# Whole products in layer 0's first projection half, seven half-size products for layer 1's last pair

## What is computed

```python
z = h @ w_in_l                       # h: 264 x 1024, w_in_l: 1024 x 4096
q, k, v, u, g = jnp.split(z, [QK_W, 2 * QK_W, 2 * QK_W + ATTN_W, 2 * QK_W + ATTN_W + POOL_W], axis=-1)
q = rms_norm(q.reshape(B, T, N_HEADS, 2, HEAD_DIM), q_gain)
k = rms_norm(k.reshape(B, T, N_HEADS, 2, HEAD_DIM), k_gain)
g = jax.nn.sigmoid(g.astype(F32)).astype(h.dtype).reshape(B, T, N_BRANCH, D_MODEL)
```

## Time and profile before

| | |
|---|---|
| median of 3 runs | 1595.51 us (1592.43 to 1597.35) |
| the profiled execution's own time | 1594.39 us |
| its span, first to last instruction | 1592.7 us |
| PE busy | 1556.1 us, 98% |
| DVE, ACT, POOL busy | 33%, 12%, 4% |
| first projection half, layer 0 | 34.42 to 102.37 us |
| first projection half, layer 1 | 481.57 to 539.03 us |
| experts of layer 1 | 697.6 to 1575 us |

### The profile page before, as it was taken

How to read it: one execution, slowest core, us unless ns; L and a number is a source line. 1 busy time by engine, 2 the same in 40 slices (tenths; PEclk the granted TensorE clock), 3 DMA queues, 4 the chain that set the end, 5 groups by cost and what they waited for, 6 DMA issues and landing times.

```text
span 1592.7 us, 38054 instructions
## 1 busy us (share of the span) xinstructions
PE 1556.1 (98%) x17094; PEld 975.9 (61%) x17094; DVE 529.0 (33%) x1244; ACT 190.8 (12%) x524; POOL 69.8 (4%) x118
## 2 busy tenths in 40 slices
PE   7999999999999999999999999999999999999997
PEld 3887798999998877944444444444444444445554
DVE  4568267656556672741101101110111011101133
ACT  3123213111112232131000000000000000000000
POOL 1115000000000110010000000000000000000010
PEclk9999999999999999999999999999999999999999
DMA  9998979786359754579999999999999999999995
GB/s 361 358 368 262 302 265 333 262 273 213 128 173 332 243 176 153 174 300 373 413 409 394 417 418 402 418 415 405 418 404 414 417 404 418 416 403 418 409 390 194
DMA packets 174360, 535.43 MB, mean 336 GB/s; under 512 B 12535, under 2 KB 101413, under 8 KB 161394
## 3 DMA queue, kind: packets, MB, share of 16 engines
q1 hardware_dynamic: 158274, 494.58, 81.2%
q0 software_dynamic: 8784, 29.03, 5.5%
q10 hardware_dynamic: 7136, 9.34, 1.8%
HBM read 517.53 MB, written 15.82 MB: 335 GB/s over the span
## 4 chain that ended last, share of the span: by engine, by line
PE 92%; DMA 4%; DVE 3%; ACT 1%; issue 1%; SPq 0%; ACTq 0%; DVEq 0%
PE banks L2107 35%; PE banks L1294 19%; PE banks L2128 17%; PE banks L1651 7%; DMA ring<-in_w_exp_up 3%; PE banks L1570 2%; PE banks L1959 2%; PE banks L1942 2%; PE banks L1786 1%; PE banks L1326 1%; PE banks L1729 1%; DMA ring<-in_w_ada 1%; ACT hT L952 0%; PE banks L1700 0%; PE banks L1496 0%
## 5 line engine op out<-in xcount | busy, mean ns | idle before, releaser
L2107 PE MATMUL banks<-ring,area 128*32 128x448 f32 x3072 | 301.8, 539 | 1.5 <-DMA ring<-in_w_exp_up 0.8
L2107 PE MATMUL banks<-ring,xT 128*32 128x448 f32 x3072 | 301.5, 539 | 1.3 <-DMA ring<-in_w_exp_up 1.3
L631 DVE TENSOR_TENSOR area<-banks,area 128x448 f32<-128x448 f32 x48 | 45.8, 954 | 572.4 <-ACT area L1252 572.4
L2128 PE MATMUL banks<-area 128*32 128x256 f32 x3840 | 226.2, 379 | 1.8 <-issue 1.8
L2107 PEld LDWEIGHTS banks<-ring,xT 128*32 128x32 f32 x3072 | 106.0, 110 | 164.4 <-issue 154.6
L2107 PEld LDWEIGHTS banks<-ring,area 128*32 128x32 f32 x3072 | 100.9, 110 | 171.1 <-issue 162.0
L2128 PEld LDWEIGHTS banks<-area 128*32 128x32 f32 x3840 | 129.3, 110 | 110.0 <-issue 46.4
L1651 PE MATMUL banks<-hT,ring 128*128 128x264 f32 x512 | 119.6, 387 | 0.0
L1252 ACT ACTIVATE area<-banks 128x448 f32<-128x448 f32 x48 | 26.1, 545 | 774.7 <-PE banks L2107 774.7
L1651 PEld LDWEIGHTS banks<-hT,ring 128*128 128x128 f32 x512 | 95.4, 190 | 17.2 <-ACT area L1072 1.3
L2128 PE MATMUL banks<-ring,area 128*32 128x256 f32 x1536 | 89.3, 379 | 0.7 <-DVE area L639 0.6
(11 more groups left out here) (375 smaller groups left out, 1322.9 us busy)
## 6 DMA issues: line engine op xcount, KB each, us to landing
ring<-in_w_exp_gate SPq DMA_DIRECT2D x128, 896.0 KB, 13.7
ring<-in_w_exp_up SPq DMA_DIRECT2D x128, 896.0 KB, 15.8
area<-in_w_exp_down SPq DMA_DIRECT2D x62, 1024.0 KB, 15.0
ring<-in_w_ada SPq DMA_DIRECT2D x96, 512.0 KB, 9.0
ring<-in_w_in SPq DMA_DIRECT2D x32, 1024.0 KB, 13.0
ring<-in_w_exp_down SPq DMA_DIRECT2D x32, 1024.0 KB
area<-in_w_exp_down SPq DMA_DIRECT2D x31, 512.0 KB
ring<-in_w_ff_gate SPq DMA_DIRECT2D x11, 1024.0 KB, 8.8
```

The lines of the kernel that those rows point to most:

```text
L631: dve.tensor_tensor(F["act_tok"][:, t, :].rearrange("p (i n) -> p n i", i=BODY), bank[3 + t][:, 0:SLICE].rearrange("p (n i) -> p n i", i=B ...
L2107: mm = pe.matmul(bank[t + 3 * half][32 * g:32 * g + 32, 0:SLICE], tokens[:, t, 32 * r:32 * r + 32], w[half][:, SLICE * g:SLICE * (g + 1)], ...
L2128: mm = pe.matmul(bank[6 + t // 2][32 * q:32 * q + 32, (t % 2) * S:(t % 2 + 1) * S], FFN["actT"][:, m % 2, t, 32 * i:32 * i + 32], wide(at) ...
```

## The change

```diff
-Z_HALVED = (1, 2, 3, 4, 5, 6, 7), (1, 2, 3, 4, 5, 6)
+Z_HALVED = (), (1, 2, 3, 4, 5, 6, 7)
```

## The result

The changed kernel takes 1596.87 us (median of 12 runs, 1595.69 to 1600.47), the kernel before, run beside it, 1594.25 us (median of 12). The ratio is 1.0017 with a 95% interval from 1.0009 to 1.0025: slower by 2.6 us, with 1.4 to 4.0 us in the interval. It is a true loss and a small one, inside the 0.3% that I had called the bound of what can be told; twelve runs beside twelve tell a little more than that. The profiled execution took 1596.72 us with a span of 1595.0, which is 2.3 us over that of before.

The account below looks back on a forecast made before the run. PE's own time was taken to bound the kernel; +4.4 - 0.7 - 0.8 = +2.9 us on the profiled 1594.39 gave 1597.3 us, as a median 1598.4 us. The range was 1594.7 to 1602 us.

Parts of the forecast that it names:

- What bounds it: Whole kernel: PE, busy 98% of the span, so the cost is roughly the difference in PE's own time.
- Layer 0's seven pairs: Layer 0's first half: pairs 1 to 7 become whole, 7.2 us each for 6.58, +4.4 us, upper end +5.7.
- Layer 1's pair 7: Layer 1's first half: pair 7 becomes halved, 6.49 us for 7.21, -0.7 us; DVE's earlier need of its page priced at nothing.
- The queries' way: Layer 0's attention: ACT copies the sample queries earlier, DVE starts the cached keys 2.6 us earlier against PE, -0.8 us.
- My copy time: Layer 0: ACT's copy of the sample queries after the change, at -15.7 us counted from the start of the gate chunks.
- The sum: Whole kernel: +4.4 - 0.7 - 0.8 = +2.9 us, forecast as a median of 1598.4 us.
- A: Layer 0: the queries' way gains nothing and gaps near their upper end; 1598.7 us on the profiled base, chance 0.13.
- B: PE's idle gap ahead of layer 1's first pair: the clock falls once more, 1.8 us, 1599.1 us; chance 0.12.
- C: Experts: their weight transfers take the delay in, -2.2 us, leaving +0.7, 1595.1 us; chance 0.13.
- D: Projection pairs: weight loads are paid beside the matmuls, so whole pairs win by 27 us net, 1569.9 us; chance 0.02.
- The signs of being wrong: PE wait in first half, layer 0 whole pair over 7.3 us, low clock outside pair 0, page wait in layer 1's pair 6.

Follow-up runs that it names:

- l0_whole: Kernel before with only layer 0's part of the change, its pairs 1 to 7 whole, layer 1 as before; 1599.28 us, ratio 1.0030.
- l1_pair7: Kernel before with only layer 1's part, pair 7 of layer 1 by seven block products, layer 0 as before; 1593.21 us, ratio 0.9993.
- q_early: Kernel before with ACT's copy of the sample queries moved ahead of its copies of pair 6, in both layers; 1592.71 us, ratio 0.9988.
- q_later: Changed kernel with layer 0's copy of the sample queries held until the first chunk of pair 7 is done; ratio 1.0011.
- split2: Changed kernel with each whole-pair matmul cut into two of 132 columns, each with its own load of the same weights; ratio 1.0020.
- split4: Changed kernel with each whole-pair matmul cut into four of 66 columns, each with its own weight load; ratio 1.0799.
- split3: Changed kernel with each whole-pair matmul cut into three of 88 columns, each with its own weight load; 1649.44 us in one timed run.

## Why the forecast held

**What bounds it** was right: PE's own time. No wait entered the first half, and l0_whole showed that a delay made there reaches the end.

**Layer 0's seven pairs** were undersized: +5.06 us for the forecast +4.4 (its upper bound was +5.7), and 7 x (7.2 - 6.58) is 4.3, not 4.4. The term that was off is the whole pair, "7.2 us", taken from layer 1. Six of the seven take 7.32 us, and the timeline of the kernel after shows where the 0.1 us lies, in the first pass of a pair:

```profile
91.39 0.39 PE L1786 MATMUL banks<-hT,ring 128*128 128x264 f32 x1
...
99.25 0.49 PE L1786 MATMUL banks<-hT,ring 128*128 128x264 f32 x1
```

The pair behind the queries' transposes starts like layer 1's pair 7 did and takes 7.22 us; the others start with a longer first pass, and take 7.32. 6 x 0.12 is the missing 0.7 us between 4.3 and 5.06. The halved pairs (6.58 us) had been read from the stretch itself, which held all their gaps; the whole pair came from another place and held only one of its two. Why the first pass is longer at some starts was not tried.

**Layer 1's pair 7**, -0.7 us: -0.71 in the changed kernel and in l1_pair7. DVE's earlier weight sums met no page that had not landed, as priced.

**The queries' way**, -0.8 us: -0.87, and by the mechanism named, which q_early showed alone and q_later in reverse. Two details were wrong. The trip of 15.6 us was taken as fixed; it is 9.9 to 15.6 us in these runs. And the value of the term depends on it, from 0 to about 1 us by the execution. My copy time (-15.7) was right (91.59 us, -15.6).

**The sum** came out at +2.6 us by the medians, for +2.9. That it is so near is in part luck. The two errors, 0.7 us of gaps and a stall that isn't there in every run, would both have raised it; the medians' interval (1.4 to 4.0 us) is too wide to say what took them back, and I leave that open. The profile's own +2.3 is +3.5 in the three stretches, +0.6 by a fall of the clock ahead of the experts, 1.9 less in the experts, and 0.1 in all the rest; the last three the forecast had at nothing.

**The rivals.** A (the queries' way gains nothing) needed a longer trip, over 18 us. DVE did not wait for the rows in the kernel after, so the trip took less than the 18.2 us from the copy at 91.59 to the first use at 109.80. B (one more fall of the clock) did not come at the gap that it named, ahead of layer 1's first pair. But the clock did fall in the kernel after, at 687 and at 1534 us, where the kernel before had it full; the first, where small products ran and no whole pair, cost 0.6 us and not B's 1.8, and the second lies in the experts and can't be told from their spread. Such falls come and go with the execution, and the spread of pair 0 of layer 0 alone is 2.7 us, as much as the whole change. One ground against B was misread: that PE had little to do before layer 0's gap. In the kernel before it was busy all the time with small products up to 32 us, at full clock:

```profile
20.00:32.00 12.00, 12.00 (x115) 5.21 (x108) 4.06 (x10) 0.48 (x1) 0.00 (x0) 1.00 1.05 395
```

C fell by l0_whole, D by split2. What D's rule missed, and my own sentence "cost grows with the columns alone" too, is the floor of 111 to 112 ns a pass: the sum was right because 132 columns are just above it.

**The signs of being wrong.** Two of the four that the forecast named came: whole pairs in layer 0 over 7.3 us (six of them, by 0.02 us, the gap above) and a low clock outside pair 0 (the two falls). No PE wait stood in the first half and no DVE wait for a page in layer 1. So the mechanism held, and the signs were set too sharp for what varies from one execution to the next.

## What to carry to other kernels

A Strassen-like split trades matmul columns for passes, and it pays only while each pass stays above the floor under a pass: here 28 matmuls of 132 columns for 16 of 264 save 0.72 us in 7.3, and by the estimate above pieces half as wide would lose. Price a group with the gaps of the place that it moves to, not of the place where it was seen. And look at what stands ahead of a small copy in an in-order queue: moving one ACT copy took away a stall of up to 1.0 us, depending on the execution, for the steady 0.7 us of the pair of layer 1, and without any change to the arithmetic. Last, before a difference of a few microseconds is put down to a change, look in both profiles for falls of the clock in stretches that it doesn't touch.

## What the runs showed of the hardware

- A float32 pass with a fresh 128x128 weight load takes 111 to 112 ns at full clock for 66 and for 88 columns (split4, split3), 112.5 for 132, and 222.5 for 264: flat up to 132 and then by the columns.
- With passes of 66 columns PE stayed at granted clock 0.50 from 60 to 120 us though it was busy 60.00 of 60.00 us; a pair took 27.5 us there and 14.44 at full clock. With passes of 88 columns the low clock lasted through nearly all of the first pair of either layer (19.36 and 19.00 us). The kernels with passes of 264 columns whose clock fell at pair 0 had it back 3.5 to 5.4 us after the pair's start. Why it stayed low was not tried.
- In or just behind PE's gaps of 2.0 us ahead of layer 0's first pair and 2.3 us ahead of the experts the clock fell in some executions and not in others: in nine of eleven at the first (the three with the gap filled not counted), in nine of fourteen at the second. At the second a fall of 3.4 us cost 0.6 to 0.8 us and one of 6.8 us 1.8.
- A round trip of 16 KB to DRAM and back, spread over 128 partitions as 2 MB, took 9.9 to 15.6 us from the copy that feeds it to its first use, in the five executions in which DVE waited for it; in three of them the instructions around it were the same, and it took 14.2 to 15.6 us.
